# Convolution inside the choice of keys, all scores first, and one rotation inside the state space's first stage

## The chip, the core and the metric

One core of a Trainium2 chip runs the whole program in one launch. The metric is device time in microseconds (us). Five engines run side by side, each through its own list of instructions in order: TensorE (PE: matrix products, into the accumulator memory PSUM), VectorE (DVE), ScalarE (ACT), GpSimd (POOL) and SyncE (SP, which here only issues transfers). They meet through semaphores; a wait holds everything behind it in that engine's list.

## The reference, cut to what matters

Two transformer blocks are computed for 1024 tokens of width 1024, in f32. Only the first half of block one is touched:

```python
proj = x @ w_in                                  # q, k, v, iq, ik, iw, z, xbc, dt_raw
q, k, iq, ik = rope(q), rope(k), rope(iq), rope(ik)
sc = sum_h relu(iq_h . ik) * iw_h                # indexer: 4 heads of 64, causal
_, sel = lax.top_k(sc, 256)                      # keys chosen for each query
att = softmax over the chosen keys of q . k, times v
xbc = silu(causal_depthwise_conv(xbc, conv_w) + conv_b)      # 4 taps
dt  = softplus(dt_raw + dt_bias);  a = -exp(a_log)
y   = chunked state space over xbc (8 chunks of 128 tokens), times silu(z), rms norm
```

## The kernel before, in words

The program is a sequence of stages (`Stage`), each closed by a barrier of all engines: the next stage's first instruction, on any engine, waits until every engine has ended the stage. What one stage leaves idle on an engine can't be used by the next. The stages that the change touches stand at the start of the program, in this order:

1. `project_index` (L728): loads the activations `xt` (feature chunks by 1024 tokens), projects chunks 4, 5 and 7 of `raw` (indexer queries and keys) and the small columns (values, indexer weights, dt).
2. `load`, called from `rotate_chunks`: a stage that only loads `turner` (a 128 by 128 matrix that swaps halves with signs), `cos` and `sin`; then `rotate` for the three index chunks. For each chunk of 128 by 1024, PE multiplies by `turner` (L314), POOL forms raw times cos (L324), DVE forms the turned times sin (L333) and adds (L338).
3. `choose_keys` (L784). PE computes for each tile t = 2..7 of 128 queries and each of four heads the scores against (t+1)*128 keys (L887; heads 0 and 2 lie in rows 0 to 63, heads 1 and 3 in rows 64 to 127), ACT takes the relu (L940), DVE weights and sums (L980, L982). Two score buffers are used in turn, so head n+2 waits for the relu of head n. Between them lie projections of all that is left: 22 groups of 8 products for the `raw` and `xbc` chunks and 8 for `z` (L876), each evicted by ACT (`keep`, L905); group i waits until group i-4 was kept. An order list interleaves them: after the scores of tiles 3, 4, 5 and 6 comes one projection each, the rest after tile 7. Then two searches run side by side: DVE finds the 256th largest score of tiles 2 to 5 bit by bit in 31 rounds (L999), ACT does the same for tiles 6 and 7, first 15 high bits (L910 to L922) and then 16 low bits of keys that DVE makes for it (`low_key`, L1041) after DVE's round b = 12. ACT keeps one projection after every second bit. At the end DVE turns the found bounds into masks (L1058 to L1067).
4. A second `load` of the same three tables, then `rotate` for chunks 0, 1, 2, 3 and 6.
5. `convolve` (L1070): taps and bias are loaded; DVE forms the four-tap sum of each of six chunks (L1093, L1095) in `conv_acc`; ACT applies silu to z (L1104) and to each sum (L1108), into a new tile `mixed`.
6. `state_space` (L1112), first stage: six small loads, then dt and the decays on DVE and ACT; PE transposes `mixed` (L1163). The second stage starts on DVE at L1363. After it comes attention over the chosen keys.

Of the kernel before, what the change touches and what calls it, by code (L numbers as in the profile page):

```python
# [27 lines left out]
P = 128  # L28
# [269 lines left out]
def rotate(book, ps, turner, cos, sin, raw, chunks, parts=P):  # L298

    nc = book.nc  # L300
    order, chunks = chunks, len(chunks)
    with ExitStack() as ctx, Stage(book, "turned_full", "cos_done", "sin_done", "rotated") as (
# [4 lines left out]
        @block.tensor  # L307
        def _(pe):
            for n in range(chunks):

                if n >= 4:
                    pe.wait_ge(sin_done, n - 3)
                for h in range(2):
                    last = nc.tensor.matmul(ps[0:parts, 2 * (n % 4) + h, :], turner[0:parts, 0:parts],  # L314
                                            raw[0:parts, order[n], tile(h, HALF)], start=True, stop=True)
                last.then_inc(full, 1)

        @block.gpsimd
        def _(pool):
            for n in range(chunks):  # L320
# [3 lines left out]
                nc.gpsimd.tensor_tensor(by_cos[0:parts, n % 2, :], raw[0:parts, order[n], :], cos[0:parts, :],  # L324
# [3 lines left out]
        def _(dve):  # L328
            for n in range(chunks):
                dve.wait_ge(full, n + 1)  # L330
                if n >= 2:
                    dve.wait_ge(rotated, n - 1)
                nc.vector.tensor_tensor(by_sin[0:parts, n % 2, :],  # L333
                                        ps[0:parts, 2 * (n % 4):2 * (n % 4) + 2, :].rearrange("p a b -> p (a b)"),
                                        sin[0:parts, :], ALU.mult).then_inc(sin_done, 1)
                dve.wait_ge(cos_done, n + 1)
                dve.wait_ge(sin_done, n + 1)
                nc.vector.tensor_tensor(raw[0:parts, order[n], :], by_cos[0:parts, n % 2, :], by_sin[0:parts, n % 2, :],  # L338
# [391 lines left out]
def project_index(book, ps, A, xt, raw, small):  # L730

    nc = book.nc
    with ExitStack() as ctx, Stage(book, "x_in0", "x_in1", "w_in", "w_rows_in", "full", "read") as (
            block, x_in0, x_in1, w_in, w_rows_in, full, read):
# [5 lines left out]
        def _(sp):  # L740
# [4 lines left out]
            sp.dma_start(wr[:, :, :], A["w_rows_small"]).then_inc(w_rows_in, 16)  # L745

# [37 lines left out]
def choose_keys(book, ps, A, xt, raw, small, xbc, z, masks, moff):  # L784
# [7 lines left out]
    pieces = [(0, 3), (3, 7), (7, M)]  # L792
    piece_of = [n for n, (a, b) in enumerate(pieces) for _ in range(a, b)]

    groups = [(m, h) for m in range(M) for h in range(2)] + [(None, t) for t in range(T)]
# [15 lines left out]
    counted = 0  # L811
    while order[counted][0] != "scores" or order[counted][1] != T - 1:
        counted += 1
    scoring, later = order[:counted + 1], [i for _, i in order[counted + 1:]]
    with ExitStack() as ctx, Stage(book, "causal_in", "w_in0", "w_in1", "w_in2", "w_z_in", "edge_zero", "projected",
                                   "kept", "full", "positive", "scored", "dve_steps", "to_count", "act_steps", "high_found", "low_ready",
                                   "low_found") as (
            block, causal_in, w_in0, w_in1, w_in2, w_z_in, edge_zero, projected, kept, full, positive, scored, steps,
            to_count, act_steps, high_found, low_ready, low_found):
# [4 lines left out]
        wz = wt[:, 0:4, :, :].rearrange("p m k c -> p (m k c)").rearrange("p (k w) -> p k w", w=ROWS_Z)  # L824
# [15 lines left out]
        summed = sb("summed_signs", [P, NA])  # L840
        taken = sb("taken_bit", [P, NA])
        low_key = ctx.enter_context(nc.sbuf_tensor("low_key", [P, NA, S], U16))

        @block.sync
        def _(sp):
            sp.dma_start(causal[:, :], A["causal"]).then_inc(causal_in, 16)
            for n, (a, b) in enumerate(pieces):
                sp.dma_start(wt[:, a:b], A["w_turned"][:, a:b]).then_inc(w_in[n], 16)

            sp.wait_ge(projected, 8)  # L850
            sp.dma_start(wz, A["w_rows_z"]).then_inc(w_z_in, 16)

# [6 lines left out]
        def _(pe):  # L859
            n = 0  # L860
            for what, i in order:
                if what == "project":
                    m, part = groups[i]

                    if i >= 4:
                        pe.wait_ge(kept, i - 3)
                    if m is None:
                        pe.wait_ge(w_z_in, 16)
                    else:
                        pe.wait_ge(w_in[piece_of[m]], 16)  # L870
                    for k in range(KD):
                        if m is None:
                            lhs, rhs = xt[:, k, tile(part)], wz[:, k, :]
                        else:
                            lhs, rhs = wt[:, m, k, :], xt[:, k, tile(part, HALF)]
                        last = nc.tensor.matmul(ps[:, 4 + i % 4, :], lhs, rhs, start=(k == 0), stop=(k == KD - 1))  # L876
                    last.then_inc(projected, 1)
                    continue
                keys = (i + 1) * P
                for h in range(IDX_HEADS):  # L880
# [9 lines left out]
                    n += 1  # L890

# [6 lines left out]
        def _(act):  # L898
            chain = Chain(act, act_steps)

            def keep(i):
# [3 lines left out]
                nc.scalar.activation(out, ps[:, 4 + i % 4, :], ACT.Copy).then_inc(kept, 1)  # L905
# [8 lines left out]
            def search(keys, edges, wanted, bits):  # L914
                for b in range(bits - 1, -1, -1):
                    count(keys, edges, summed)
                    for n in range(NA):
                        ins = nc.scalar.activation(taken[:, n:n + 1], summed[:, n:n + 1], ACT.Sign,
                                                   bias=wanted[:, n:n + 1])
# [5 lines left out]
                    if b % 2 == 0 and later:  # L925
# [3 lines left out]
            for what, i in scoring:  # L929
                if what == "project":  # L930
                    keep(i)
                    continue
# [2839 lines left out]
```

## Time and profile before

| | us |
|---|---|
| median of 3 runs (4019.55 to 4021.31) | 4021.19 |
| the profiled execution's own time | 4022.54 |
| its span in the trace | 4020.8 |

| engine | busy in the whole span | share |
|---|---|---|
| PE | 3451.8 | 86% |
| DVE | 2697.5 | 67% |
| ACT | 2020.0 | 50% |
| POOL | 519.3 | 13% |

The page's shares are averages over the program; most of it (from about 490 us on) is attention, experts and block two, which this change leaves as they are. So the reading goes by the timeline of the first 412 us. There a row is: start in us from the span's start, duration, engine, source line, operation, written tile<-read tiles, shapes, count, and in brackets the idle time before it with what ended it. Rows of equal kind that follow each other closely are merged, with one duration for all. "PEclk" in a table of windows is the granted TensorE clock: 1.00 is 2.4 GHz, 0.50 is 1.2 GHz, something between is a stretch with both.

### The profile page before, as it was taken

What the parts mean: (1) busy time and instruction counts of PE and PEld (TensorE: products, weight loads), DVE (VectorE), ACT (ScalarE), POOL (GpSimd) and SP (SyncE); (2) the same over time, 40 slices, a digit from 0 to 9 for tenths busy, and PEclk for the clock granted to TensorE, in tenths of its full rate; (3) what the DMA queues carried; (4) which work ended last, traced back from release to release, by engine and by line L of the source; (5) the groups of instructions that cost most, each with busy time, mean ns of one, the idle gap of its engine ahead of it and who ended that gap; (6) DMA issues with size and microseconds to landing.
All of it is one profiled execution on the core that took longest, in us unless ns stands there. A gap on an engine that the chain in (4) does not pass through costs nothing. (4 is left out here: it accounts for less than half of the span.)

```text
span 4020.8 us, 54279 instructions
## 1 busy us (share of the span) xinstructions
PE 3451.8 (86%) x18166; PEld 2550.1 (63%) x18166; DVE 2697.5 (67%) x4385; ACT 2020.0 (50%) x3303; POOL 519.3 (13%) x365
## 2 busy tenths in 40 slices
PE   7994798678854998999689999879989995999994
PEld 3442467566643875467568888669655674888883
DVE  1695664689975237566489999741655646999995
ACT  0571363156643146444167777531554432777774
POOL 0001300045543100100001111110000000111110
PEclk9997799789986999999789999989999996999997
DMA  2100002366534110101389999731100034999996
GB/s 100 53 1 17 1 1 96 138 230 247 191 120 176 48 38 11 38 1 64 147 301 389 383 383 382 270 115 42 28 22 27 1 111 173 362 390 383 382 383 224
DMA packets 122141, 650.37 MB, mean 162 GB/s; under 512 B 14048, under 2 KB 22624, under 8 KB 69984
## 3 DMA queue, kind: packets, MB, share of 16 engines
q1 hardware_dynamic: 101504, 573.48, 36.8%
q0 software_dynamic: 15984, 58.20, 5.0%
q10 hardware_dynamic: 4464, 16.25, 1.0%
q8 instruction: 108, 1.77, 0.2%
q14 instruction: 81, 0.66, 0.1%
HBM read 585.50 MB, written 62.39 MB: 161 GB/s over the span
## 5 line engine op out<-in xcount | busy, mean ns | idle before, releaser
L3302 DVE TENSOR_TENSOR low_ring<-mix,high_ring 128x2048 fp32r<-128x2048 f32 x256 | 576.6, 2284 | 41.3 <-ACT high_ring L3251 41.3
L3251 ACT ACTIVATE high_ring<-mix 128x2048 fp32r<-128x2048 f32 x256 | 477.9, 1938 | 80.3 <-PEq L125 80.3
L3192 PE MATMUL ps<-high_ring,x_high 128*128 128x512 f32 x1024 | 410.0, 400 | 15.0 <-DVE low_ring L3302 7.6
L3193 PE MATMUL ps<-low_ring,x_high 128*128 128x512 f32 x1024 | 401.2, 392 | 0.0
L3194 PE MATMUL ps<-high_ring,x_low 128*128 128x512 f32 x1024 | 400.6, 391 | 0.0
L3302 DVE TENSOR_TENSOR low_ring<-more_raw,high_ring 128x2048 fp32r<-128x2048 f32 x128 | 290.1, 2286 | 28.0 <-ACT high_ring L3251 28.0
L3251 ACT ACTIVATE high_ring<-more_raw 128x2048 fp32r<-128x2048 f32 x128 | 246.7, 1927 | 0.0
L3192 PEld LDWEIGHTS ps<-high_ring,x_high 128*128 128x128 f32 x1024 | 193.2, 189 | 79.0 <-DVE low_ring L3302 20.5
L3194 PEld LDWEIGHTS ps<-high_ring,x_low 128*128 128x128 f32 x1024 | 193.1, 189 | 41.4
L3193 PEld LDWEIGHTS ps<-low_ring,x_high 128*128 128x128 f32 x1024 | 193.3, 189 | 37.6
L3192 PE MATMUL ps<-high_ring,h_high 128*128 128x512 f32 x512 | 205.2, 401 | 0.0
L3194 PE MATMUL ps<-high_ring,h_low 128*128 128x512 f32 x512 | 200.0, 391 | 0.0
L3193 PE MATMUL ps<-low_ring,h_high 128*128 128x512 f32 x512 | 199.3, 389 | 0.0
L2760 DVE TENSOR_TENSOR w_unit_low<-mix,w_unit_high 128x1024 fp32r<-128x1024 f32 x32 | 40.5, 1281 | 231.0 <-ACT w_unit_high L2693 231.0
L2391 DVE TENSOR_TENSOR up_low<-raw_experts,up_high 128x1024 fp32r<-128x1024 f32 x124 | 181.6, 1485 | 14.1 <-ACT up_high L2310 13.6
L665 ACT ACTIVATE probs<-ps,less 128x1024 f32<-128x1024 f32 x96 | 106.9, 1114 | 158.9 <-DVE less L701 158.9
L607 PE MATMUL ps<-qk_body,q_mla 96*128 96x512 f32 x384 | 180.5, 593 | 1.7 <-PEq L125 1.7
L3160 POOL DMA_INDIRECT residual<-out_e,add_to x32 | 89.3, 2790 | 693.0 <-DVE out_e L3341 693.0
L3146 POOL COPY take_from<-slot_index 128x1 uint32 (+1 forms) x32 | 38.8, 1213 | 980.2 <-POOLq L125 721.6
L294 PE MATMUL ps<-w_high,mix_high 128*128 128x512 f32 x384 | 154.4, 402 | 9.2 <-DVE w_low L1869 9.2
L876 PE MATMUL ps<-xt,wt 128*128 128x512 f32 x352 | 155.5, 602 | 3.0 <-ACT xbc L905 3.0
L468 ACT ACTIVATE probs<-logits,less 128x384 f32<-128x384 f32 (+7 forms) x224 | 153.5, 690 | 8.0 <-DVE mix L545 5.7
(492 smaller groups left out, 8143.0 us busy)
## 6 DMA issues: line engine op xcount, KB each, us to landing
mix<-in_expert_units SPq DMA_DIRECT2D x256, 1024.0 KB, 8.0
more_raw<-in_expert_units SPq DMA_DIRECT2D x128, 1024.0 KB, 8.8
raw_experts<-in_expert_units SPq DMA_DIRECT2D x16, 3072.0 KB, 11.7
expert_out<-out ACTq DMA_DIRECT2D x31, 512.0 KB, 3.3
mix<-in_w_turned SPq DMA_DIRECT2D x20, 512.0 KB, 4.0
feats<-residual SPq DMA_DIRECT2D x16, 512.0 KB, 7.5
qk_tail<-in_w_out SPq DMA_DIRECT2D x8, 1024.0 KB, 8.2
mix<-residual SPq DMA_DIRECT2D x16, 512.0 KB, 3.3
```

The costliest lines, as they stand in the source:

```text
L294: last = nc.tensor.matmul(out, left, right, start=(n == 0), stop=(n == len(terms) - 1))
L468: nc.scalar.activation(probs[:, p % 2, i, 0:pair["keys"]], logits[:, p % 2, i, 0:pair["keys"]], ACT.Exp, scale=scale, bias=less[:, p % 4, ...
L607: nc.tensor.matmul(ps[:, 2 * (n % 2) + b, :], q[0:MLA_D, h, tile(t)], k[0:MLA_D, h, tile(b, HALF)], start=True, stop=True).then_inc(scores ...
L665: nc.scalar.activation(probs[:, n % 2, :], source, ACT.Exp, scale=scale, bias=less[:, n % 4:n % 4 + 1], accum_out=total[:, p % 4, i:i + 1] ...
L876: last = nc.tensor.matmul(ps[:, 4 + i % 4, :], lhs, rhs, start=(k == 0), stop=(k == KD - 1))
L2391: nc.vector.tensor_tensor(up_low[:, n:n + 1, :], up_raw(slot, n), up_high[:, n:n + 1, :].bitcast(F32), ALU.subtract).then_inc(up_low_ready, 1)
L3160: pool.indirect_dma_start(sum_dram, bass.IndirectOffsetOnAxis(ap=add_to[:, 0:1], axis=0), out[:, :], None, compute_op=ALU.add).then_inc(su ...
L3192: nc.tensor.matmul(ps[:, bank, :], left_high, high, start=first, stop=False)
L3193: nc.tensor.matmul(ps[:, bank, :], left_high, low, start=False, stop=False)
L3194: return nc.tensor.matmul(ps[:, bank, :], left_low, high, start=False, stop=final)
L3251: nc.scalar.activation(w_high[:, n % RING, :], raw[n % RAW_UNITS], ACT.Copy).then_inc(high_ready, 1)
L3302: nc.vector.tensor_tensor(w_low[:, n % RING, :], raw[n % RAW_UNITS], w_high[:, n % RING, :].bitcast(F32), ALU.subtract).then_inc(low_ready, 1)
```

## The change

- `load` is gone from both rotations. The tables are kept: `turner` in its own tile, `cos` and `sin` in the first four tiles' second half of `heads_out` (named `ssd`, not yet written then), loaded by `project_index`. They are read as two halves of 512, with a step between.
- In `choose_keys` all scores come first, then the 30 projections, the `xbc` chunks ahead of the `raw` ones and `z` last. DVE convolves chunk m ahead of its rounds b = 26, 23, 20, 18, 16 and 14, waiting until both halves of the chunk were kept; the sum goes back into `xbc` itself (in place), with `acc` in a free part of `heads_out`. ACT keeps a projection after two bits of three (was: one of two), `low_key` is made after round b = 17 (was 12), and after its search ACT applies silu to the six `xbc` chunks, between the last projections; `z` gets silu as it is kept.
- The stage `convolve` is gone, and `state_space` reads `xbc` in place of `mixed`. Its constants are loaded in `choose_keys`.
- The rotation of chunks 0, 1, 2, 3 and 6 has no stage of its own: its operations are put between those of the state space's first stage, with PSUM banks 6 and 7 as its only buffer; the transposes have six banks left (were eight).

The core of the diff:

```diff
-def project_index(book, ps, A, xt, raw, small):
+def project_index(book, ps, A, xt, raw, small, meanwhile):
...
             sp.dma_start(wr[:, :, :], A["w_rows_small"]).then_inc(w_rows_in, 16)
+            for to, what in meanwhile:
+                sp.dma_start(to, what).then_inc(tables_in, 16)
+            sp.wait_ge(tables_in, 16 * len(meanwhile))
...
-    order = []
-    done = 0
-    for t in range(2, T):
-        order.append(("scores", t))
-        if t >= 3:
-            order.append(("project", done))
-            done += 1
-    order += [("project", g) for g in range(done, len(groups))]
+    chunk_order = list(range(FIRST, M)) + list(range(FIRST))
+    groups = [(m, h) for m in chunk_order for h in range(2)] + [(None, t) for t in range(T)]
+    convolve_before = {26: 0, 23: 1, 20: 2, 18: 3, 16: 4, 14: 5}
...
+        low_key = spare[:, 2:2 + NA, :].bitcast(U16)
+        acc = spare[:, 0:2, :]
...
-                nc.scalar.activation(out, ps[:, 4 + i % 4, :], ACT.Copy).then_inc(kept, 1)
+                nc.scalar.activation(out, ps[:, 4 + i % 4, :], ACT.Silu if m is None else ACT.Copy).then_inc(kept, 1)
...
-                    if b % 2 == 0 and later:
+                    if b % 3:
                         keep(later.pop(0))
...
             act.sem_inc(low_found, 1)
+            act.wait_ge(taps_in, 16 * (2 + len(meanwhile)))
+            for m in range(XBC_CHUNKS):
+                if later:
+                    keep(later.pop(0))
+                act.wait_ge(summed, m + 1)
+                nc.scalar.activation(xbc[:, m, 0:S], xbc[:, m, 0:S], ACT.Silu, bias=tap_bias[:, m:m + 1])
...
+            def convolve(m):
+                taken = halves(xbc[:, m, 0:S])
+                dve.wait_ge(kept, 2 * m + 2)
+                chain.step(nc.vector.tensor_scalar(acc, halves(xbc[:, m, 1:1 + S]), taps[:, m, 1:2], None, ALU.mult))
+                for j in range(2, CONV):
+                    chain.step(nc.vector.scalar_tensor_tensor(out=acc, in0=halves(xbc[:, m, j:j + S]),
+                                                              scalar=taps[:, m, j:j + 1], in1=acc, op0=ALU.mult,
+                                                              op1=ALU.add))
+                nc.vector.scalar_tensor_tensor(out=taken, in0=taken, scalar=taps[:, m, 0:1], in1=acc, op0=ALU.mult,
+                                               op1=ALU.add).then_inc(summed, 1)
...
             for b in range(30, -1, -1):
+                if b in convolve_before:
+                    convolve(convolve_before[b])
...
-                if b == 12:
+                if b == 17:
                     dve.wait_ge(high_found, 1)
...
+                def turn_chunk(n):
+                    if n >= 1:
+                        pe.wait_ge(sin_done, n)
+                    for h in range(2):
+                        last = nc.tensor.matmul(ps[:, 6 + h, :], turner[:, :], raw[:, order[n], tile(h, HALF)],
+                                                start=True, stop=True)
+                    last.then_inc(turned_full, 1)
```

On PE the end of the scoring in `choose_keys` reads, before (L887 are scores, L876 projections; `ps` is PSUM):

```order
L887 MATMUL ps<-raw 128x384
L876 MATMUL ps<-xt,wt 128x512 x8
L887 MATMUL ps<-raw 128x512 x8
L876 MATMUL ps<-xt,wt 128x512 x144
L876 MATMUL ps<-wt,xt 128x512 x64
L125 UNCONDITIONAL_BRANCH
```

and now (L892 are scores, L879 projections):

```order
L892 MATMUL ps<-raw 128x384
L892 MATMUL ps<-raw 128x512 x8
L879 MATMUL ps<-xt,wt 128x512 x176
L879 MATMUL ps<-wt,xt 128x512 x64
L125 UNCONDITIONAL_BRANCH
```

The four projections between the tiles (8 products each) went behind the last score: 144 products became 176, and PE has nothing to do beside the scores while it waits for ACT.

On DVE in `state_space`, first stage, there stood before (dt, its sign and absolute value, and 1 + exp of it):

```order
L1198 TENSOR_TENSOR dt<-small,dt_bias 128x64
L1199 TENSOR_SCALAR u<-dt 128x64
L1200 TENSOR_TENSOR u<-u,dt 128x64
L1203 TENSOR_SCALAR u<-u 128x64
L1206 TENSOR_SCALAR u<-u 128x64
L1207 TENSOR_SCALAR cum<-u 128x64
L1208 TENSOR_TENSOR u<-u,cum 128x64
```

and now (`heads_out` holds the sines here; the 128x1024 rows are the rotation's):

```order
L1206 TENSOR_TENSOR dt<-small,dt_bias 128x64
L1207 TENSOR_SCALAR u<-dt 128x64
L1208 TENSOR_TENSOR u<-u,dt 128x64
L1196 TENSOR_TENSOR by_sin<-ps,heads_out 128x1024
L1212 TENSOR_SCALAR u<-u 128x64
L1202 TENSOR_TENSOR raw<-by_cos,by_sin 128x1024
L1196 TENSOR_TENSOR by_sin<-ps,heads_out 128x1024
L1217 TENSOR_SCALAR u<-u 128x64
L1218 TENSOR_SCALAR cum<-u 128x64
L1219 TENSOR_TENSOR u<-u,cum 128x64
```

Three operations of the rotation stand ahead of L1217, the first operation that waits for the logarithm. The other seven follow: two behind the last operation of dt, five behind the cumulative sums.

## Rows read from the trace of the kernel before

**Rows 1.** Timeline, start of the program; columns: start us, us, engine line op, tiles

```profile
73.67 0.34 SPq L3490 DMA_DIRECT2D turner<-in_turner  x1
...
79.55 7.40 PE L314 MATMUL ps<-raw,turner 128*128 128x512 f32 x12 [6.77 <-PEq L125]
...
83.34 1.22 DVE L333 TENSOR_TENSOR by_sin<-ps,sin 128x1024 f32<-128x1024 f32 x1 [83.20 <-PE ps L314]
...
84.67 1.22 DVE L338 TENSOR_TENSOR raw<-by_cos,by_sin 128x1024 f32<-128x1024 f32 x1
...
85.98 2.35 POOL L324 TENSOR_TENSOR by_cos<-raw,cos 128x1024 f32<-128x1024 f32 x1 [1.70 <-DVE raw L338]
...
87.14 2.27 DVE L338 TENSOR_TENSOR raw<-by_cos,by_sin 128x1024 f32<-128x1024 f32 x1
```

**Rows 2.** Timeline, TensorE in the scoring of choose_keys (L887)

```profile
92.19 1.65 PE L887 MATMUL ps<-raw 64*128 64x384 f32 x4 [5.24 <-PEq L125]
...
96.61 2.45 PE L887 MATMUL ps<-raw 64*128 64x512 f32 x4 [0.20 <-ACT relu L940]
...
99.37 2.56 PE L887 MATMUL ps<-raw 64*128 64x512 f32 x4 [0.31 <-ACT relu L940]
...
110.02 1.36 PE L887 MATMUL ps<-raw 64*128 64x512 f32 x8
...
112.15 1.94 PE L887 MATMUL ps<-raw 64*128 64x512 f32 x8 [0.78 <-ACT relu L940]
...
145.13 1.99 PE L887 MATMUL ps<-raw 64*128 64x512 f32 x8
...
148.23 2.90 PE L887 MATMUL ps<-raw 64*128 64x512 f32 x8 [1.10 <-ACT relu L940]
```

**Rows 3.** Windows; columns: stretch, length, busy by engine, PEclk, DMA share, GB/s

```profile
92.00:102.00 10.00, 8.76 (x17) 3.42 (x17) 4.33 (x11) 3.35 (x8) 0.12 (x1) 0.50 0.84 328
...
104.00:106.00 2.00, 2.00 (x5) 0.83 (x5) 0.04 (x1) 0.00 (x0) 0.00 (x0) 0.98 0.99 426
...
145.00:151.00 6.00, 4.90 (x17) 1.86 (x16) 2.04 (x2) 3.29 (x4) 0.00 (x0) 1.00 0.00 0
...
495.00:510.00 15.00, 15.00 (x67) 7.93 (x66) 6.05 (x33) 7.45 (x29) 0.00 (x0) 0.50 0.01 2
```

**Rows 4.** Timeline, ScalarE: search starts, one bit of it, the last projection kept

```profile
161.86 1.04 ACT L910 ACTIVATE relu<-masks,edge_high 128x896 bf16<-128x896 int16 x1 [3.03 <-DVE masks L1022]
...
165.67 1.03 ACT L910 ACTIVATE relu<-masks,edge_high 128x896 bf16<-128x896 int16 x1
...
168.99 1.04 ACT L910 ACTIVATE relu<-masks,edge_high 128x896 bf16<-128x896 int16 x1
...
335.01 0.60 ACT L905 ACTIVATE heads_out<-ps 128x512 f32<-128x512 f32 x1 [6.27 <-PE ps L876]
```

**Rows 5.** Timeline, VectorE: scores end, loop starts, loop over, stage over

```profile
154.01 0.29 DVE L988 TENSOR_TENSOR masks<-masks,causal 128x128 f32<-128x128 f32 x1
...
163.57 0.67 DVE L999 TENSOR_SCALAR_CACHE_REDUCE relu<-masks,edge,less_wanted 128x384 bf16<-128x384 f32 x1
...
280.53 0.16 DVE L1054 TENSOR_TENSOR bound<-edge,sign 128x4 f32<-128x4 f32 x1
...
319.03 0.69 DVE L1067 TENSOR_SCALAR masks<-relu 128x1024 f32<-128x1024 f32 x1
```

**Rows 6.** Timeline, VectorE in convolve: first operation of two chunks following each other

```profile
364.50 0.75 DVE L1093 TENSOR_SCALAR conv_acc<-xbc,taps 128x1024 f32<-128x1024 f32 x1 [2.58 <-DMA conv_bias<-in_conv_b]
...
369.13 0.75 DVE L1093 TENSOR_SCALAR conv_acc<-xbc,taps 128x1024 f32<-128x1024 f32 x1
```

**Rows 7.** Timeline, VectorE: first stage of the state space, start of the second

```profile
401.80 0.22 DVE L1198 TENSOR_TENSOR dt<-small,dt_bias 128x64 f32<-128x64 f32 x1 [9.46 <-DMA hidden<-in_hidden]
...
411.13 0.22 DVE L1224 TENSOR_TENSOR u<-u,cum 128x64 f32<-128x64 f32 x1
...
412.24 1.27 DVE L1363 TENSOR_TENSOR a_upto<-upto,adt 128x1024 f32<-128x1024 f32 x1 [0.89 <-PEq L125]
```

More of the change, by code:

```diff
@@ L313, in _ @@
                 for h in range(2):
-                    last = nc.tensor.matmul(ps[0:parts, 2 * (n % 4) + h, :], turner[0:parts, 0:parts],
-                                            raw[0:parts, order[n], tile(h, HALF)], start=True, stop=True)
+                    last = nc.tensor.matmul(ps[:, 2 * (n % 4) + h, :], turner[:, :], raw[:, order[n], tile(h, HALF)],
+                                            start=True, stop=True)
                 last.then_inc(full, 1)
@@ L727, in _ @@
             write(N // 2 - 1)
[L730 removed]
+def project_index(book, ps, A, xt, raw, small, meanwhile):
     nc = book.nc
[L733 to L734 removed]
+    with ExitStack() as ctx, Stage(book, "x_in0", "x_in1", "w_in", "w_rows_in", "full", "read",
+                                   "tables_in") as (
+            block, x_in0, x_in1, w_in, w_rows_in, full, read, tables_in):
         x_in = [x_in0, x_in1]
@@ L781, in _, with choose_keys @@
                 g += 1
-def choose_keys(book, ps, A, xt, raw, small, xbc, z, masks, moff):
+def choose_keys(book, ps, A, xt, raw, small, xbc, z, masks, moff, spare, meanwhile):
     nc = book.nc
@@ L810, in choose_keys @@
     HIGH_BITS, LOW_BITS = 15, 16
[L811 to L814, printed above, removed]
+    later = list(range(len(groups)))
     with ExitStack() as ctx, Stage(book, "causal_in", "w_in0", "w_in1", "w_in2", "w_z_in", "edge_zero", "projected",
                                    "kept", "full", "positive", "scored", "dve_steps", "to_count", "act_steps", "high_found", "low_ready",
-                                   "low_found") as (
+                                   "low_found", "taps_in", "summed") as (
             block, causal_in, w_in0, w_in1, w_in2, w_z_in, edge_zero, projected, kept, full, positive, scored, steps,
-            to_count, act_steps, high_found, low_ready, low_found):
+            to_count, act_steps, high_found, low_ready, low_found, taps_in, summed):
         w_in = [w_in0, w_in1, w_in2]
@@ L859, in _, with project @@
         def _(pe):
-            n = 0
[L861 to L878, printed above, removed]
+            def project(i):
+                m, part = groups[i]
+                if i >= 4:
+                    pe.wait_ge(kept, i - 3)
+                if m is None:
+                    pe.wait_ge(w_z_in, 16)
+                else:
+                    pe.wait_ge(w_in[piece_of[m]], 16)
+                for k in range(KD):
+                    if m is None:
+                        lhs, rhs = xt[:, k, tile(part)], wz[:, k, :]
+                    else:
+                        lhs, rhs = wt[:, m, k, :], xt[:, k, tile(part, HALF)]
+                    last = nc.tensor.matmul(ps[:, 4 + i % 4, :], lhs, rhs, start=(k == 0), stop=(k == KD - 1))
+                last.then_inc(projected, 1)
+            n = 0
+            for i in tiles:
                 keys = (i + 1) * P
@@ L890, in _ @@
                     n += 1
+            for i in range(len(groups)):
+                project(i)
         score = [masks[:, moff[t]:moff[t] + (t + 1) * P] for t in tiles]
@@ L924, in search @@
                     chain.step(ins)
-                    if b % 2 == 0 and later:
+                    if b % 3:
                         keep(later.pop(0))
             n = 0
[L929 to L932, printed above, removed]
+            for i in tiles:
                 keys = (i + 1) * P
@@ L3434, in block_one @@
                 z = heads_out[:, :, 0:HALF]
-                def rotate_chunks(chunks):
-                    with ExitStack() as part:
-                        turner = sb(part, f"turner_{book.count}", [P, P])
-                        cos = sb(part, f"cos_{book.count}", [P, S])
-                        sin = sb(part, f"sin_{book.count}", [P, S])
-                        load(book, [(turner[:, :], A["turner64"]), (cos[:, :], A["cos64"]), (sin[:, :], A["sin64"])])
-                        rotate(book, ps, turner, cos, sin, raw, chunks)
+                turner = sb(early, "turner", [P, P])
```

177 lines of the change are left out of this document (92 added, 85 removed).

## The prediction, made before the changed kernel ran

> **What bounds the kernel now.** I read first the page's slices, which show that the first tenth of the span, where the change lies, is not like the rest: a chain of stages, each waiting for the one before. So I went on in the timeline, stage by stage, looking only for what ends last. In `choose_keys` (92.19 to 335.61) it is TensorE: ScalarE keeps the last projection at 335.01 + 0.60 after 6.27 idle, waiting for PE [rows 4], while DVE has been done since 319.03 + 0.69 = 319.72 [rows 5]. From 335.61 to 412.24, where the state space's second stage starts on DVE [rows 7], stand 76.6 us of load, rotation, convolution, load and dt, in which PE has almost no work. At the start of the program PE waits 6.77 us for a load stage [rows 1]. Two spacings set the pace of `choose_keys`: a projection group takes PE 0.60 + 6.27 = 6.87 us at the full clock, which is 0.86 for each of its 8 products of 512 columns [rows 4]; and of the scores, two heads take one cycle of PE and relu, since head n+2 waits for the relu of head n. That cycle is (96.61 - 92.19)/2 = 2.21 us for 384 keys, 2.76 for 512, 2.13 for 640 and 3.10 for 1024 [rows 2]. It is shorter for 640 than for 512 because the granted clock was 0.50 up to the first projections and 0.98 two microseconds into them [rows 3].
>
> **Part 1, the tables loaded early.** The first load issue is at 73.67 and PE's first product at 79.55 [rows 1]; without the load stage the rotation starts at about 73.4, 6.1 earlier. PE has then only just ended the small projections, and a chunk's two products take 2 x 0.86 plus some 0.3 of latency, 2.0, where the row shows 83.34 - 79.55 = 3.8. Against that, POOL's first product (2.35) no longer lies ahead of DVE's addition but beside it, and such an addition takes 2.27 and not 1.22 [rows 1]. I take 1 us net for both, bounds 0 and 2: scoring starts at 85.2 and not at 92.19, **-7.0**. The loads themselves follow `wr_small` and have some 50 us of projections as cover.
>
> **Part 2, all scores first.** What is removed is nothing: PE has the same 48 score products and 30 groups. What counts is what PE does in the waits. Before, PE scored from 92.19 to 151.13, with four projections inside (about 29.4 of it, four times the 6.87 and some 2 more at the low clock), so 29.6 for scores alone. Now there is no full-height product among the scores. Whether the clock rises is the question that decides this case. The rows: 10 us of scores with PE busy 8.76 of them stay at 0.50; the projections lift it at once; the attention's half-height products and transposes stay at 0.50 for 15 us with PE shown busy all the time [rows 3]. Where the clock had been lifted by projections it stays at 1.00 through the scores of tile 7. So I take 0.50 throughout. At half clock a cycle grows by its keys x 4 passes / 2400, which is 0.86 per 512 columns as above: 2.13 + 1.07 = 3.20 (640), 3.10 + 1.71 = 4.81 (1024), and for 768 and 896 between them 3.7 and 4.3. Twice 2.21 + 2.76 + 3.20 + 3.7 + 4.3 + 4.81 is 42.0, and PE ends at 85.2 + 42 = 127.2.
>
> The Trainium skill, "TensorE: Matmul & The Clock Gate", Part 1, says that the low clock is the default and that activity of the engine releases it; its own products count as activity, without a word on half-height ones. By that the scores would run at 2.4 GHz soon after their start; the first two rows named above speak against it, and it is the second case below.
>
> Then the 30 groups: 30 x 6.87 = 206.1, plus about 1.1 until the clock has risen, plus 0.6 for the last keep: 335.0. No group waits for a keep, by this count of the other two engines:
> - ACT: its search starts 7.6 after the scores' end on DVE (154.30 to 161.86 [rows 4, 5]). DVE ends 3.2 after PE (154.30 against 151.13), so at 130.5; ACT starts at 138. A bit takes 3.32 (165.67 to 168.99), a keep at most 0.6 [rows 4]. 15 bits and 10 keeps would be 56 us, but keep 10 needs group 10, projected at 128.3 + 11 x 6.87 = 203.9; high_found at 208.
> - DVE: 9.3 after the scores' end the loop starts (154.30 to 163.57), at 139.8. Loop and `low_key` took 280.53 - 163.57 = 117.0, 3.70 a round with 2.2 for `low_key` [rows 5]; a chunk's convolution 369.13 - 364.50 = 4.63 [rows 6], six of them 28. `low_key` comes at 139.8 + 14 x 3.70 + 4 x 4.63 = 210, just behind high_found. ACT's 16 low bits and 10 keeps end, held once more by PE, near 277. DVE's loop ends at 139.8 + 117.0 + 27.8 = 284.6, the stage's DVE part 39.2 later (280.53 to 319.72) [rows 5] at 323.8.
>
> So the convolution lies wholly under the projections, with 11 us to spare, and PE bounds the stage as before. Silu of six chunks on ACT (1024 columns, like a count of the search at 1.03 to 1.3) is between keeps 6.87 apart. The stage ends at 335.0 where it was 335.61, 7.0 later counted from its start: scores at the low clock take back what the early tables gave. **+6.4** beside the -7.0.
>
> **Part 3, the three stages that go.** From 335.61 to 412.24 stood 76.6. What stays is one stage, counted from its start S, in DVE's list. POOL works beside it (2.35 a chunk), so I give an addition 2.27 wherever POOL may run. 0.7 for dt; by_sin(0) when PE has turned chunk 0, 2.0 to 3.3; add(0) to 5.9; by_sin(1) needs PE's turn, queued behind eight transposes, and two copies of ACT, which first loads the logarithm's table: to 8.3; ten small operations in 3.0; add(1) and by_sin(2) to 14.8; four small operations on the sums, the last of them the row at 411.13, to 15.8; add(2), then two chunks of 1.22 + 2.27 with PE's turn of 2 us ahead of each, since banks 6 and 7 are one buffer: to 25.0. With 0.9 for the two barriers' crossings the second stage starts 25.9 after the old one's end: **-50.7**. Bounds: 20 (PE and DVE overlap better, no contention) and 34 (low clock for PE, 4.0 a turn, or every small operation held by POOL). The constants' 9.46 us wait for DMA [rows 7] goes, since they come in `choose_keys`; `hidden`, needed in the second stage only, has the whole first one.
>
> The Trainium skill, "GPSIMD Engine Reference", section 8, says that POOL shares its SBUF interfaces with VectorE, in conflict with operations of two SBUF inputs. The trace agrees: 2.27 beside POOL, 1.22 without. The new stage has seven small operations of that kind, which lie under 0.3 us each and are held by up to one POOL product if the rule is strict: that belongs to the upper bound.
>
> **Sum.** -7.0 + 6.4 - 50.7 = -51.3 against the profiled execution's 4022.54, which is 3971.2; its span is 4020.8, the rest lies around it and stays. It stands 1.35 above the median of the runs shown, so **3970 us**.
>
> **Cases.**
> 1. Forecast (chance 0.52): the clock is low through most of the scores: 3964 to 3979, from the bounds of parts 1 and 3.
> 2. The clock rises during the scores, or never falls before them (0.38). For it: PE's idle time between rotation and scores is 5.24 [rows 2], and tile 7 keeps PE busier at the low clock (4.4 of 4.8) than tile 3 did. Against it: rows 3. If it rises at tile 6, the four cycles there cost 2 x (1.5 + 1.7) = 6.4 less: 3964. If it is high from tile 4 on, as before, the scores take 29.6: 3957.6.
> 3. DVE or ACT becomes the bound of `choose_keys` (0.06): the waits of DVE for keeps and of ACT for `low_key` (ACT idled for it before, too) would have to grow by over 11 us, or the 24 operations on views with a step run half as fast again: +5 to +15, 3975 to 3985.
> 4. Slower (0.02): the clock stays at 0.50 into the projections, now that they are one block behind a low-clock stretch. Each group then costs 6.87 more, and both searches wait with it. It turns the result from the eighth such group on; all 30 would be +206, 4176. Against it: two microseconds of projections lifted the clock at 102 to 104 [rows 3].
> 5. The change saves nothing (0.02): the removed stages would have to be under other work. They aren't, the barriers see to that.
>
> Faster by over 0.2% (8 us, about what a measurement of this kernel can tell from no change) in cases 1 to 3: 0.97. Within 0.2%: 0.01. Slower: 0.02. Range for 8 in 10: from 3955 (case 2 with its end and 2 us for the stage of part 3) to 3979 (case 1's upper end).
>
> **What would show it.** The rotation's first product on PE near 73.4 and the first score near 85. PEclk over the scores: 0.50, and the last score's relu near 128; if it is 1.00, near 116. `choose_keys` ends on a keep of z that waits for PE, DVE done 11 us before. Projections 6.87 apart, with no stall on `kept`. From that end to the first a_upto 26 us, in which DVE waits for PE's turns. Wrong I am if DVE ends `choose_keys`, if ACT's keeps stall PE, or if the first stage of the state space takes over 34 us.

## The result, and the profile after

| | before | after |
|---|---|---|
| median, us (4 runs each, one chip) | 4021.25 (4019.55 to 4024.64) | 3971.05 (3967.48 to 3972.41) |
| profiled execution, its span | 4022.54, 4020.8 | 3972.41, 3970.6 |
| first score | 92.19 | 86.83 |
| `choose_keys`, first score to stage end | 243.4 | 247.5 |
| stage end to the first a_upto | 76.6 | 27.5 |
| first a_upto to the end of the span | 3608.6 | 3608.8 |

The ratio is 0.9872 (95% interval 0.9859 to 0.9884): faster by 50.2 us. In the trace the four last lines of the table give -5.4 + 4.1 - 49.1 + 0.2 = -50.2, the whole difference of the spans; the work itself is the same (the page has PE busy 3458.7 us and DVE 2698.4, before 3451.8 and 2697.5; PE's 7 more are scores at the low clock). The first score isn't fixed to the microsecond: in ten more profiles of kernels that are the same up to there it comes at 85.27 to 87.21.

The stretch that was [rows 1], on PE and then on DVE:

```profile
69.76 4.41 PE L772 MATMUL ps<-wr_small,xt 128*128 128x76 f32 x38
74.74 5.39 PE L318 MATMUL ps<-raw,turner 128*128 128x512 f32 x12 [0.58 <-PEq L125]
86.83 1.65 PE L892 MATMUL ps<-raw 64*128 64x384 f32 x4 [6.70 <-PEq L125]
```

```profile
78.07 2.47 DVE L341 TENSOR_TENSOR raw<-by_cos,by_sin 128x1024 f32<-128x1024 f32 x1
81.78 2.27 DVE L341 TENSOR_TENSOR raw<-by_cos,by_sin 128x1024 f32<-128x1024 f32 x1
85.28 1.23 DVE L341 TENSOR_TENSOR raw<-by_cos,by_sin 128x1024 f32<-128x1024 f32 x1
```

The rotation starts 0.58 after the small projections; the additions beside POOL's products take over 2.2, the last one, alone, 1.23. The first scores of tile 5, both rows of tile 7 (eight products a row) and the first projections, to be held against [rows 2]; then the windows, against [rows 3]:

```profile
103.35 3.52 PE L892 MATMUL ps<-raw 64*128 64x512 f32 x8 [0.20 <-ACT relu L944]
...
119.72 4.20 PE L892 MATMUL ps<-raw 64*128 64x512 f32 x8 [0.20 <-ACT relu L944]
124.61 2.90 PE L892 MATMUL ps<-raw 64*128 64x512 f32 x8 [0.70 <-ACT relu L944]
127.44 7.99 PE L879 MATMUL ps<-xt,wt 128*128 128x512 f32 x18
```

```profile
95.00:105.00 10.00, 9.30 (x24) 5.80 (x22) 5.14 (x8) 3.69 (x6) 0.00 (x0) 0.50 0.89 359
105.00:115.00 10.00, 9.50 (x23) 4.82 (x19) 4.46 (x7) 3.63 (x5) 0.00 (x0) 0.50 0.00 0
115.00:125.00 10.00, 8.80 (x18) 3.80 (x18) 4.77 (x6) 4.31 (x6) 0.00 (x0) 0.58 0.01 2
125.00:128.00 3.00, 3.00 (x10) 1.18 (x9) 1.95 (x3) 1.84 (x3) 0.00 (x0) 1.00 0.00 0
140.00:335.00 195.00, 194.06 (x453) 85.78 (x452) 178.82 (x395) 124.51 (x293) 0.37 (x1) 1.00 0.03 11
```

The columns of a window are its span, the busy time (and count) of PE, PEld, DVE, ACT and POOL, then PEclk, the DMA share and GB/s. PE is over 90% busy at 0.50 from 95 to 115, and the clock rises at 123.4, within the scores of tile 7. From 140 to 335 PE is busy for 194.06 of 195.

The end of the stage on ACT (against [rows 4]) and on DVE (against [rows 5]), and one convolution on DVE within the search (against [rows 6]):

```profile
333.74 0.60 ACT L912 ACTIVATE heads_out<-ps 128x512 f32<-128x512 f32 x1 [6.27 <-PE ps L879]
```

```profile
154.75 0.76 DVE L1040 TENSOR_SCALAR heads_out<-xbc,taps 128x1024 f32<-128x1024 f32 x1
155.54 2.61 DVE L1042 SCALAR_TENSOR_TENSOR heads_out<-xbc,taps,heads_out 128x1024 f32<-128x1024 f32 x2
158.18 1.28 DVE L1045 SCALAR_TENSOR_TENSOR xbc<-xbc,taps,heads_out 128x1024 f32<-128x1024 f32 x1
...
323.20 0.69 DVE L1092 TENSOR_SCALAR masks<-relu 128x1024 f32<-128x1024 f32 x1
```

The last keep waits 6.27 for PE as before; DVE is done 10.5 earlier (323.89 against 334.34). Then the one stage that replaced four, on DVE (against [rows 7]), and what POOL does beside it:

```profile
334.64 2.41 DVE L1206 TENSOR_TENSOR dt<-small,dt_bias 128x64 f32<-128x64 f32 x1 [10.75 <-PEq L125]
337.09 2.25 DVE L1207 TENSOR_SCALAR u<-dt 128x64 f32<-128x64 f32 x1
...
339.51 1.22 DVE L1196 TENSOR_TENSOR by_sin<-ps,heads_out 128x1024 f32<-128x1024 f32 x1
...
346.10 1.23 DVE L1196 TENSOR_TENSOR by_sin<-ps,heads_out 128x1024 f32<-128x1024 f32 x1 [4.04 <-PE ps L1134]
...
351.31 1.22 DVE L1196 TENSOR_TENSOR by_sin<-ps,heads_out 128x1024 f32<-128x1024 f32 x1
352.44 0.21 DVE L1234 COPY cum<-ps 128x64 f32<-128x64 f32 x1
352.69 1.18 DVE L1235 TENSOR_SCALAR less_cum<-cum 128x64 f32<-128x64 f32 x1
...
361.82 1.27 DVE L1380 TENSOR_TENSOR a_upto<-upto,adt 128x1024 f32<-128x1024 f32 x1 [0.32 <-PEq L125]
```

```profile
334.63 4.66 POOL L1166 TENSOR_TENSOR by_cos<-raw,heads_out 128x1024 f32<-128x1024 f32 x2 [247.72 <-POOLq L125]
342.14 2.35 POOL L1166 TENSOR_TENSOR by_cos<-raw,heads_out 128x1024 f32<-128x1024 f32 x1 [2.86 <-DVE raw L1202]
351.47 2.35 POOL L1166 TENSOR_TENSOR by_cos<-raw,heads_out 128x1024 f32<-128x1024 f32 x1 [6.98 <-DVE raw L1202]
```

Two small operations of 64 columns, which take 0.2 in the stage of before, take 2.41 and 2.25; they end at 337.05 and 339.34, and POOL's two products at about 336.96 and 339.29. `less_cum` ends at 353.87, POOL's third at 353.82. The rows that read PSUM (by_sin at 351.31, the copy at 352.44) keep 1.22 and 0.21 beside that product.

### The profile page after: what moved, and what is told of

Same layout as the page of the kernel before. It is cut to its first block and busy times, and to the rows that moved or that the text cites. A ratio compares the mean times of both kernels' runs of the same rounds, so it can differ in the third digit from the quotient of the medians.

```text
span 3970.6 us, 54231 instructions
## 1 busy us (share of the span) xinstructions
PE 3458.7 (87%) x18166; PEld 2555.1 (64%) x18166; DVE 2698.4 (68%) x4385; ACT 2013.8 (51%) x3295; POOL 522.4 (13%) x365
## 5 line engine op out<-in xcount | busy, mean ns | idle before, releaser
L2408 DVE TENSOR_TENSOR up_low<-raw_experts,up_high 128x1024 fp32r<-128x1024 f32 x124 | 182.4, 1491 | 15.2 <-ACT up_high L2327 14.7
L699 DVE TENSOR_REDUCE top<-ps 128x1 f32<-128x512 f32 x192 | 132.5, 690 | 34.6 <-PE ps L610 34.6
```

The costliest lines, as they stand in the source:

```text
L699: ins = nc.vector.tensor_reduce(top[:, n % 2, b:b + 1], ps[:, 2 * (n % 2) + b, :], AX.X, ALU.max)
L2408: nc.vector.tensor_tensor(up_low[:, n:n + 1, :], up_raw(slot, n), up_high[:, n:n + 1, :].bitcast(F32), ALU.subtract).then_inc(up_low_ready, 1)
```

## The experiments

Totals move by 5 to 14 us between the runs of one kernel (the changed kernel: 3961 to 3972 over two sets), so the steps are read between bounds in the profiled executions, one for each kernel, and the medians are given beside them. Only e5, e6 and e7 have intervals clear of both of the changed kernel's (after and e11), and e3 of one; what the others show, their profiles show. Where the state space's first stage is the same (after, e11, e1, e2, e3), the stretch up to a_upto takes 26.1 to 28.9, so a gain or loss of 1 or 2 us in it is read from its rows. Each ratio is against the kernel before on the same chip.

| kernel | median (ratio, 95% interval) | clock 1.00 from | first score to stage end | stage end to a_upto |
|---|---|---|---|---|
| after | 3971.05 (0.9859 to 0.9884) | 123.4 | 247.5 | 27.5 |
| e11, the same again | 3966.64 (0.9840 to 0.9873) | 117.9 | 245.7 | 28.1 |
| e1, one group between | 3967.51 (0.9852 to 0.9882) | 96.9 | 238.4 | 28.7 |
| e2, extra products | 3971.78 (0.9855 to 0.9886) | 99.2, lost 109.4 to 119.7 | 249.7 | 28.9 |
| e3, four groups between | 3977.46 (0.9875 to 0.9903) | 97.2 | 255.1 | 26.1 |
| e4, POOL later | 3969.56 (0.9855 to 0.9885) | 122.9 | 247.5 | 26.7 |
| e5, tables only | 4005.08 (0.9954 to 0.9978) | 97.8 (104.4 in before) | 243.5 | 68.3 |
| e6, scores first only | 4029.62 (1.0010 to 1.0029) | 129.6 | 253.7 | 76.4 |
| e7, convolution apart | 3996.94 (0.9929 to 0.9956) | 124.0 | 247.5 | 59.0 |
| e8, rotation apart | 3967.41 (0.9854 to 0.9885) | 107.1 | 241.2 | 30.4 |
| e9, e1 and e10 together | 3968.34 (0.9848 to 0.9880) | 98.2 | 238.6 | 28.9 |
| e10, another stage order | 3969.54 (0.9856 to 0.9889) | 107.2 | 241.2 | 28.0 |
| e12, DVE alone | 3964.60 (0.9837 to 0.9870) | 118.4 | 245.7 | 25.5 |

**e1: one projection between the scores of tiles 3 and 4.**

```diff
+    BETWEEN = {3: 0}
...
+                if i in BETWEEN:
+                    project(BETWEEN[i])
...
+                if i in BETWEEN:
+                    keep(later.pop(0))
```

> The changed kernel, with one of the 30 projections moved back between the scores of tiles 3 and 4. Theory (the low clock is what scores first costs): that full-height group lifts TensorE's clock, tiles 4 to 7 are scored at 2.4 GHz and stay there. PE's last score at about 125.5 and 29 groups behind it instead of 30: choose_keys ends at about 325.3 where it ended at 334.3, -9 us, about 3962. DVE then ends only 3 us before. Rival (half-height scores alone can't hold the high clock): PEclk falls back to 0.50 within tile 4 or 5, and the time stays at 3971.

The clock rose with the group at 96.9 and stayed to the end of the scores; the same eight products of tile 5 that took 3.52 take 2.15:

```profile
94.94 8.07 PE L880 MATMUL ps<-xt,wt 128*128 128x512 f32 x16
107.22 2.15 PE L893 MATMUL ps<-raw 64*128 64x512 f32 x8 [0.20 <-ACT relu L947]
```

```profile
97.00:124.00 27.00, 24.70 (x80) 11.81 (x79) 14.15 (x19) 12.82 (x17) 0.00 (x0) 1.00 0.20 77
```

The stage is 9.1 us shorter: its scores take 30.4 without the group, 40.7 in after, so the low clock over the scores is what "scores first" costs. The medians don't show the gain (3967.51 against 3971.05 and 3966.64), and of e1's four runs only one was profiled, the fastest (3963.11, mean clock 0.932). The slowest (3972.12) has 0.929, as after's runs have (0.929 and 0.930), so the group may not keep the clock up in every execution.

**e2: eight extra products there, whose result is never read** (PE works some 7 us more).

```diff
+                if i == 3:
+                    pe.wait_ge(w_in[0], 16)
+                    for k in range(KD):
+                        nc.tensor.matmul(ps[:, 7, :], wt[:, FIRST, k, :], xt[:, k, 0:HALF], start=(k == 0),
+                                         stop=(k == KD - 1))
```

> The changed kernel in its own order, with eight extra full-height products (their result is never read) between the scores of tiles 3 and 4. It does 7 us more work on PE than the changed kernel. Theory (clock): the scores of tiles 4 to 7 save some 9 to 10 us at 2.4 GHz, so it is still 2 us faster, about 3969. Rival (what counts is only where the projections stand): 7 to 8 us slower, about 3978.

A miss: the clock rose and was lost again after the two rows of tile 4.

```profile
106.93 1.94 PE L892 MATMUL ps<-raw 64*128 64x512 f32 x8 [0.78 <-ACT relu L949]
109.07 11.16 PE L892 MATMUL ps<-raw 64*128 64x512 f32 x24 [0.20 <-ACT relu L949]
```

```profile
103.00:108.00 5.00, 4.22 (x17) 2.02 (x17) 0.97 (x2) 1.30 (x2) 0.00 (x0) 1.00 0.18 57
110.00:119.00 9.00, 9.00 (x21) 3.96 (x20) 5.15 (x8) 3.25 (x4) 0.00 (x0) 0.50 0.00 0
```

In e1 the same rows (101 to 106) have PE busy for the same 4.22 of 5.00, and there the clock held. After such a group, half-height scores can keep it or lose it. The profiled execution is also the slowest of e2's four (3975.62, mean clock 0.930; the others 0.932 and 0.933), so the loss need not be in the others, of which there are no profiles.

**e3: the four groups of the old order**, at tiles 3 to 6, as before the change.

```diff
+    BETWEEN = {3: 0, 4: 1, 5: 2, 6: 3}
```

> The changed kernel with the order of before in the scoring: one projection after each of tiles 3, 4, 5 and 6. PE would end choose_keys at about 325, 9 us sooner. Theory (by the same counts as in the prediction): DVE gets the last score only at about 149, and 9.3 + 117.0 + 27.8 + 39.2 later is 342: DVE becomes the bound of the stage, +8 us, about 3979. Rival (PE bounds the stage in any order): -9 us, 3962.

```profile
323.20 0.60 ACT L915 ACTIVATE heads_out<-ps 128x512 f32<-128x512 f32 x1 [5.23 <-PE ps L880]
```

```profile
340.11 0.69 DVE L1097 TENSOR_SCALAR masks<-relu 128x1024 f32<-128x1024 f32 x1
```

The last keep of a projection now ends at 323.80, and DVE ends the stage at 340.80, 17 later: its search starts only behind the last score. Here DVE is the bound, and the stage is 7.6 longer than after's. That is what the order "scores first" is worth once DVE also convolves.

**e4: POOL's products start only after exp(-|x|) is asked for** (one added wait).

```diff
             def _(pool):
+                pool.wait_ge(exp_x, 1)
```

> The changed kernel, with POOL's first product of the state space's first stage waiting for the three small DVE operations on dt. Theory (POOL holds DVE's small operations through the shared SBUF interface: 2.41 and 2.25 us where they took 0.22 and 0.20): they take 0.2 each again, ACT's copies start 2.9 us sooner, and all that follows: about 3968.2. Rival (the stage is bound by PE's turns or by POOL's own products, which now start 0.8 us later): no change or +0.8.

dt and its negative are back at 0.23 and 0.20, but POOL's product now meets the next operation, which was 0.18:

```profile
334.24 0.23 DVE L1207 TENSOR_TENSOR dt<-small,dt_bias 128x64 f32<-128x64 f32 x1 [10.78 <-PEq L125]
337.37 2.37 DVE L1213 TENSOR_SCALAR u<-u 128x64 f32<-128x64 f32 x1
```

The stall moved. The stretch is 0.8 us shorter where 2.9 were expected, no more than it moves by itself. That dt is fast right behind the barrier here says that the barrier was not what slowed it.

**e5: before, with the tables loaded early and both `load` stages gone**; all else as before.

> The kernel before with one part of the change alone: the tables are loaded by project_index and both load stages are gone. Theory (the stages are a chain, so each load stage counts in full): -5.4 at the first (scoring starts at 86.8 and not at 92.2) and -7.4 at the second (6.6 of load, 0.8 for a first turn at the high clock): 4008.4. Rival (part of it is taken back by POOL and DVE in each other's way or by table loads beside the first weights): -8 to -10.

The first score comes at 85.77 and the stretch to a_upto is 68.3 instead of 76.6; the spans differ by 17.6, the medians by 16.7, and 14.7 lie in these two places, 1.9 more than the 12.8 expected.

**e6: before, with the scores first and nothing else.**

```diff
     for t in range(2, T):
         order.append(("scores", t))
-        if t >= 3:
-            order.append(("project", done))
-            done += 1
```

> The kernel before with another part alone: all scores ahead of all projections. Theory (the clock stays at 1.2 GHz while only scores run): scoring takes 40.7 us where scores alone took 29.6, PE's stage end moves from 335.6 to 339.6, and to about 344 where ACT's keeps (one of two bits, one in 7.15 us) fall behind PE: +4 to +9, about 4029. Rival (scores first is free or a gain, since DVE starts its search 18 us earlier): 4021 or below.

```profile
125.80 4.25 PE L884 MATMUL ps<-raw 64*128 64x512 f32 x8 [0.20 <-ACT relu L937]
130.69 2.90 PE L884 MATMUL ps<-raw 64*128 64x512 f32 x8 [0.64 <-ACT relu L937]
133.52 1.98 PE L873 MATMUL ps<-xt,wt 128*128 128x512 f32 x4
```

The stage is 10.3 longer than before's: PE is its bound, so it pays the low clock and gains nothing. By itself this part is a loss (1.0010 to 1.0029). It also shows a part of the change that has no experiment of its own. The scores take 40.7 as in after, yet the stage is 6.2 longer, since PE waits once for a keep of ACT (3.0, and half of the 6.8 at the low clock behind it):

```profile
226.07 9.20 PE L873 MATMUL ps<-xt,wt 128*128 128x512 f32 x14 [3.02 <-ACT raw L902]
```

From 225.2 to 232 the granted clock is 0.50. Before has the same wait (3.02 at 243.60, then 0.50 to 247.4); after, where ACT keeps a projection after two bits of three, has none. That the new pace of the keeps is what removed it fits, but no run has it alone.

**e7: after, with the convolution as a stage of its own** (in place as well, taps loaded there), and **e8: after, with the rotation as a stage of its own** (no load). The call that each adds, e7's first (what they take out elsewhere is left out here):

```diff
+                convolve(book, A, xbc, ssd[:, 4:6, :])
```

```diff
+                rotate(book, ps, turner, cos, sin, raw, OTHER_CHUNKS)
```

> The changed kernel with the convolution (in place) as a stage of its own again, behind choose_keys, taps loaded in it. Theory (the convolution is wholly hidden under projections): choose_keys keeps its length, and the stage costs 2.3 for the taps, six times 4.63 and a last silu of 1.15: +31.6, about 4002.6. Rival (the convolution stretched choose_keys): choose_keys gets shorter, and the whole costs less than +31.

> The changed kernel with the rotation of chunks 0, 1, 2, 3 and 6 as a stage of its own again, without a load. Theory: that stage takes 18.8 us (first turn 2.0, 9.8 for three chunks, 3.5 for each more) and the first stage of the state space 10.4 without it, 29.5 with the barrier against 27.2 together: +2.3, about 3973.4; the merge itself hides little, since DVE is the engine that both need. Rival (the merge hides the rotation): +10 to +18.

e7: 59.0 from stage end to a_upto, +31.5 (by the medians 26): 3.5 for the taps (338.11 against the stage end at 334.64), 28.5 for six sums of 4.75, 1.2 for the last silu, less 1.6 in the state space's first stage, where PE's second turn, for one, meets the high clock and takes 1.88, not 2.95. DVE ends `choose_keys` 11.5 earlier than in after, and the stage itself is not shorter: the convolution is free there. e8: +2.9 against after, +1.5 against the longest of the others (28.9). The median of e8 is no higher than after's, since the scores took 34.3 and not 40.7; the clock rose at 107.1:

```profile
103.64 3.52 PE L892 MATMUL ps<-raw 64*128 64x512 f32 x8 [0.20 <-ACT relu L944]
107.46 2.25 PE L892 MATMUL ps<-raw 64*128 64x512 f32 x8 [0.31 <-ACT relu L944]
```

**e10: another order in the first state-space stage**: the turn of chunk 1 two transposes earlier, and POOL held until u + 1 is written. **e9** is e10 with e1's group (of `xbc`; its expectation calls it one of z).

```diff
-                    if g == 8:
+                    if g == 6:
                         turn_chunk(1)
...
             def _(pool):
+                pool.wait_ge(one_more, 1)
```

> The changed kernel with three edits: one projection of z between the scores of tiles 3 and 4; the rotation of chunk 1 in the first state-space stage emitted at its seventh step instead of its ninth, so that its chain ends earlier; POOL's products by the cosine begin only after u + 1 is written. If one projection lifts the clock as in the run with one group (stage of the choice 238.4 us against 247.5) and the first stage loses its last rotation chain behind the chunk sum (27.5 us to a_upto before, 23 to 25 after), the time is 3957 to 3962. Rival: the higher clock is lost again within the scores, as it was with the eight extra products, and the small operations of VectorE are held by another POOL product: then 3967 to 3972, no gain.

> The same two edits of the first state-space stage without the projection between scores. Theory: the stretch from the end of the choice of keys to a_upto falls from 27.5 us to 23 to 25, because the rotation of chunk 1 no longer ends after the sums of the chunk, and dt and u + 1 are written at 0.2 us each instead of being held 2.3 us each. Rival: VectorE's total in the stretch bounds it and only the order changes: 26 to 27.5. The time of the whole moves by that, 3966 to 3968 or 3971, unless the clock rises elsewhere in the scores.

Both expectations of a gain were missed: e9's total is 3968.34 (its rival, 3967 to 3972), and e10's stretch is 28.0, just above its rival's 26 to 27.5. The stall is now in the addition, which first waits for POOL's first product and then runs beside its second:

```profile
334.49 3.38 DVE L1203 TENSOR_TENSOR raw<-by_cos,by_sin 128x1024 f32<-128x1024 f32 x1 [2.48 <-POOL by_cos L1167]
338.93 1.42 DVE L1218 TENSOR_SCALAR u<-u 128x64 f32<-128x64 f32 x1
```

```profile
332.10 4.70 POOL L1167 TENSOR_TENSOR by_cos<-raw,heads_out 128x1024 f32<-128x1024 f32 x2 [244.80 <-DVE u L1213]
337.95 2.35 POOL L1167 TENSOR_TENSOR by_cos<-raw,heads_out 128x1024 f32<-128x1024 f32 x1 [1.16 <-DVE raw L1203]
```

The addition ends at 337.87; less its own 1.22 that is 336.65, POOL's second product ends at about 336.80. L1218 ends at 340.35, POOL's third at 340.30. e9 kept the clock, and its stage is 238.6; but its first state-space stage was 28.9, and its part behind a_upto 3612.4, where the others have 3605.1 to 3612.2 without a visible cause. Its total is no better than after's.

**e11: the changed kernel again**, beside e9 and e10.

> The changed kernel again, on the same chip as the two others, to see how far the scoring of one and the same program moves with the moment at which the clock rises. It took 40.7 us with the rise 36 us after its first product. If that moment is free, as 20 us in the run with the rotation as a stage of its own suggests, the scoring takes 34 to 41 us here, and the median is 3965 to 3973. If it is fixed by the program, the scoring is within 0.5 us of 40.7.

The clock rose at 117.9, 5.5 earlier than in the first profile, and the scores took 38.8 instead of 40.7. One program, another moment.

**e12: DVE makes the five products by the cosine itself; POOL is idle.**

```diff
+                def by_cosine(n):
+                    if n >= 2:
+                        dve.wait_ge(rotated, n - 1)
+                    nc.vector.tensor_tensor(halves(by_cos[:, n % 2, :]), halves(raw[:, order[n], :]), cos,
+                                            ALU.mult).then_inc(cos_done, 1)
```

> The changed kernel with POOL out of the first state-space stage: VectorE itself makes the five products of raw and cos (the first while it waits for TensorE's first turn, the others ahead of their turns). Theory (VectorE and POOL exclude each other when both work on SBUF alone, each VectorE operation of that kind waiting until POOL's product ends): the stretched rows go back to their plain times, dt 2.41 to 0.23, its negative 2.25 to 0.20, less_cum 1.18 to 0.20, the addition of chunk 3 from 2.27 to 1.22, which is 6.3 us together; the five products cost 5 x 1.22 = 6.1, of which some 3 lie in VectorE's waits for TensorE. From the end of the choice of keys to a_upto 24 to 25.5 instead of 27.5, total 3968 or a rise of the clock away from it. Rival (the first operations after a barrier are slow by themselves): the rows keep 2.4 and 2.25, and the stretch becomes 30 or more.

```profile
332.02 0.23 DVE L1206 TENSOR_TENSOR dt<-small,dt_bias 128x64 f32<-128x64 f32 x1 [10.76 <-PEq L125]
332.29 0.20 DVE L1207 TENSOR_SCALAR u<-dt 128x64 f32<-128x64 f32 x1
332.66 1.22 DVE L1187 TENSOR_TENSOR by_cos<-raw,heads_out 128x1024 f32<-128x1024 f32 x1
...
346.43 0.20 DVE L1236 TENSOR_SCALAR less_cum<-cum 128x64 f32<-128x64 f32 x1
...
350.72 1.23 DVE L1202 TENSOR_TENSOR raw<-by_cos,by_sin 128x1024 f32<-128x1024 f32 x1
...
357.17 1.27 DVE L1381 TENSOR_TENSOR a_upto<-upto,adt 128x1024 f32<-128x1024 f32 x1 [0.32 <-PEq L125]
```

Every stretched row is at its plain length, behind the barrier too, so the rival fell. The stretch is 25.5, 2.0 less than in after, though DVE does five products more; it is under all of the 26.1 to 28.9, but by 0.6 at the least. Its median is the lowest of all, 2 to 6 us below the changed kernel's two (3971.05 and 3966.64), near what the totals vary by. So the rows show what POOL costs DVE; that the stretch gains by its absence is likely, its size open.

## Why the prediction was right

It said 3970 (3955 to 3979), and the time was 3971.05. Step by step:

- **Part 1, -7.0, was -5.4.** The mechanism and its price held: from the end of the small projections to the first score it is 12.7 where it was 19.4, 6.7 less, and the same 12.7 in e5 and e11. The other 1.4 is the program's start: the small projections ended at 74.16 where before has 72.78, and over the fourteen profiles, whose work on PE is the same up to there, that end lies from 72.6 to 74.5.
- **Part 2, +6.4, was +4.1.** The mechanism held: low clock, PE as the bound, projections without a gap (30 of them in 206.9), DVE done 10.5 before, by the forecast 11. The scores took 40.7 and not 42.0, and the 1.1 for the rise of the clock was not due. e1 and e6 show the low clock's price, 9 to 10, and e3 the late start of DVE's search without this order, +7.6 net.
- **Cases 1 and 2 were no rivals.** I gave 0.52 to a low clock through the scores and 0.38 to a rise within them. Both are the same program: it rose at 123.4 and at 117.9 in two profiles of it, and at 107 in e8 and e10, whose instructions up to there are the same. The range was right to hold both; the sharp odds were not, and which of the two an execution shows is luck as far as the forecast goes.
- **Part 3, -50.7, was -49.1**, 27.5 and not 25.9. The term that was mis-sized is POOL's price, in both directions. I wrote that small operations are held by up to one product "if the rule is strict" and left that to the upper bound. It is strict: dt, its negative and less_cum take 2.41 + 2.25 + 1.18 for what e12 shows to be 0.23 + 0.20 + 0.20, 5.2 us. Against that, I priced all five additions at 2.27, and four of them took 1.22 or 1.23, 4.2 us less. Along the path, counted from the stage's start, by_sin(1) ended at 13.0 and not 8.3 (8.2 in e12), the operations on the sums at 20.0 and not 15.8, the last addition at 27.2 and not 25.0. That the total is only 1.6 off is two errors that cancel; 1.6 is also within what this stretch moves by from profile to profile (26.1 to 28.9).
- The parts of the 49.1: e7 puts the convolution's move at 31.5, e5 the tables' at 8.3, e8 the rotation's merging at only 2.9. The 6.4 that are left have no run of their own; what else went there is the wait for the state space's constants (9.46 in before).
- The sum, -51.3 against -50.2, is nearer than its parts, which are off by +1.6, -2.3 and +1.6.
- Cases 3 to 5 did not come about; e3 shows case 3's condition (DVE ends the stage) one edit away.

The Trainium skill, "SBUF — State Buffer", section "SBUF: two separate sides", says of the pair of ports that VectorE and POOL share that it is an exclusive lock, held for the whole instruction by whoever starts first. The rows above agree for POOL holding VectorE: held small operations end when POOL's product does, and by_sin or the copies, which read PSUM, take 1.22 and 0.21 beside it. Two of the three held ones (the negative of dt, less_cum) read one tile only, so the prediction's kind, two SBUF inputs, was too narrow. Whether VectorE holds POOL no row shows: its products took 2.35 each, and I find none that starts within such an operation. Taken at that word, the strict price would have been the forecast of part 3 and not its upper bound.

## What to carry to other kernels

Find for each stage who ends it, and by how much: 28 us of convolution on DVE cost nothing in a stage that PE ends (DVE is still 10.5 early), and 31.5 in a stage of its own. An order that is best for the engine that waits may take full-height work out from between half-height products and cost the clock; e1 and e9 show that one full group can be enough, e2 that it need not be. When POOL is given work "beside" VectorE, count each operation of VectorE on SBUF alone as standing behind it: at 2.35 against 1.22 for the same product, POOL brought nothing in this stretch (26.1 to 28.9 with it, 25.5 without). And look at the engine that empties PSUM: one wait of 3.02 for a keep cost PE the full clock as well.

## What the hardware showed that was not expected

- The clock can rise over half-height products, late and at no fixed time: 32 and 37 us after the first score for one program (e11, after), 32 in e12, 37 in e4, e6 and e7, 20 in e8 and e10, with PE shown 88% to 95% busy in after's windows from 95 us on. It goes with how long before the first score the clock had fallen: 4.1 to 4.5 us where it is 37 (e6, another program up to there, apart), 3.9 where it is 20, 1.7 to 2.0 where it is 32. That is an order in seven profiles; no run tests it. The Trainium skill, "TensorE: Matmul & The Clock Gate", Part 1, has activity of the engine release the low clock. The full-height group did so (1.9 us after its start in e1, 2.8 in e2); the half-height products came to it only 20 to 37 us after their first.
- The clock can be lost with PE 84% busy (4.22 of 5.00 in e2, then 0.50 for 10 us), and kept with the same rows at the same 4.22 of 5.00 (e1).
- A product on POOL holds DVE's operations on SBUF alone until it ends: 0.20 became 2.25, 1.22 became 3.38.
- The start of the program varies too: the first small projection begins at 58.2 to 60.1 us in the fourteen profiles.
- The part behind a_upto, the same instructions in all, took 3605 to 3612 us between executions. What moves it stays open.
